# First MLP, parts of five strips, first strip pair: groups behind five plain pieces and two apart, where they stood behind four and three apart

## The chip, the cores and the metric

The kernel runs on one core of a Trainium2 chip (trn2). Five engines work from queues of their own: TensorE (PE) multiplies, VectorE (DVE), ScalarE (ACT) and GpSimd (POOL) work on elements, and SyncE (SP) issues most DMAs. They wait for each other through semaphores. The metric is the device time of one execution in microseconds (us).

## What is computed

The reference chains two blocks over 256 tokens of width 2048, all in fp32. The change lies in the MLP of the first block, in its second matrix:

```python
def sq_relu_mlp(h, w1, w2):
    return jnp.square(jax.nn.relu(h @ w1)) @ w2

# first_block, DEPTH = 1, D_MODEL = 2048, D_FF = 8192:
    h = h + y                                   # y: attention with stick-breaking weights
    h = h + sq_relu_mlp(rms_norm(h, norm_mlp[i]), mlp_w1[i], mlp_w2[i])
return rms_norm(h, final_norm)
# second_block: local attention and pooling, then a gated MLP with a convolution (w_up, w_down)
```

## The kernel before

**Pieces.** Every weight matrix is cut into pieces of 256 rows by 512 columns. A *plain* piece is loaded into one of six `raw` buffers (512 KB). ACT copies it to `Wh`, rounded to the matrix format (the high half, line 1132), and DVE subtracts to get `Wl`, the low half (line 1356). The activations lie there as high and low halves too. PE then issues three products for each of 2 row halves and 2 blocks of 128 rows: 12 matmuls of 128x512 to a plain piece. The products of a strip (512 columns) add up in one PSUM set, `ps0` or `ps1`.

**Groups.** In a *strip pair*, two neighbouring strips of `mlp_w2`, some rows are done for both strips together, as a product of 2x2 blocks with seven multiplications. The function is `seven`. Such a group stands in the list of pieces as four quarters, q0 to q3 (kinds `s0` to `s3`), with 6, 6, 6 and 3 matmuls. q0 and q1 have a raw buffer each, q2 and q3 have no load of their own: DVE makes them from the two raw buffers, by four sums (lines 1362 to 1367, buffer `wsum`). Mixed tokens (`hidMix`) are the other factor, and part of the result goes to a third PSUM set, `ps2`. When the last group is done, `fold` and `fold_rest` add `ps2` into `xN` on DVE, with one copy on ACT.

**The order.** The planner writes a list of pieces (`p.pieces`) and from it one list of steps, which all engines follow, each with its own part. While PE is at piece i, the piece four further on is split (`LEAD` = 4, there are `NW` = 5 buffers for `Wh` and `Wl`). For q0 that split brings the four sums with it (`sums_and_split`). Jobs put off with `later(n, ...)` come n plain pieces further on; a quarter counts as half a piece, the last one as a quarter of it.

**The first MLP.** The hidden width is done in three parts of 6, 5 and 5 strips. Each part first computes its strips of `mlp_w1`, then multiplies them with its rows of `mlp_w2`, in two strip pairs (s4 = 0 and s4 = 2). A part of five strips has ten pieces of rows; three of them are groups (`sevens`) and seven are plain in each of the two strips, a and b: a0 to a6, b0 to b6. In the first pair the last two of each (a5, a6, b5, b6) stand at the end as a tail (`tail` = 2), as their rows are those of the last hidden strip.

A hidden strip takes a way round before it can be multiplied: ACT takes it out of PSUM with ReLU and squares it (`stage_rows`, lines 1192 and 1200, into `T0`), SP writes it to memory and lands it turned (`land_rows`), DVE transposes it from `T0` to `T1` (`turn_strip`, line 1459), ACT writes its high half (`hid_high`, line 1235), DVE its low half (`hid_low`, line 1524). `T0` is one buffer, so ACT can take the next strip out of PSUM only behind the transpose of the one before. In the first pair, a3 and a4 read the fourth hidden strip of the part (tiles 12 to 15), the tail reads the fifth.

**Where the groups stand.** `strip_pair` puts `lead` plain pieces of strip a first, and then groups with `gap` plain pieces between them:

```python
lead, gap = (lead or 4, 3 if lead is None or len(plain) > 7 else 2) if tail else (lead or 2, 3 if len(plain) > 7 else 2)
rest = a[lead:n] + b[:n] if tail else a[lead:n - 1] + b[:lead] + a[n - 1:] + b[lead:]
```

For the first pair of a part of five strips (no `lead` given, seven plain pieces, n = 5) this gives a0 a1 a2 a3, group, a4 b0 b1, group, b2 b3 b4, group, a5 a6 b5 b6.

Of the kernel before, what the change touches and what calls it, by code (L numbers as in the profile page):

```python
# [26 lines left out]
class Plan:  # L27
# [7 lines left out]
    def done(self, name, by=1):  # L35

        if name not in self.sems:
            self.sems[name], self.count[name] = self.sem(f"s_{name}"), 0
        self.count[name] += by
        return self.sems[name], self.count[name]  # L40

    def step(self, kind, **kw):
        self.steps.append(dict(kind=kind, **kw))
        return self.steps[-1]

    def after(self, i, job, ahead=False):
        jobs = self.later_steps.setdefault(i, [])
        jobs.insert(0 if ahead else len(jobs), job)

    def later(self, n, job):  # L50

        i, left = self.at, 4 * n
        while left > 0:
            i += 1
            left -= QUARTERS.get(self.pieces[i]["kind"], 4) if i < len(self.pieces) else 4
        self.after(i, job)


def plan_program(sem):
# [34 lines left out]
    def strip(w, col, ks, mov, tiles, evac, koff=0):  # L94
        first = len(p.pieces)
        strips[0] += 1
        for n, kp in enumerate(ks):
            src = (w, "rows", kp * 256, col)
            p.pieces.append(dict(src=src, shape=2, mov=mov, kt=2 * (kp - koff), tiles=tiles, kind="N", first=n == 0,
                                 start=(n == 0, n == 0), last=n == len(ks) - 1, evac=evac, early=None, strip=strips[0]))  # L100
        return first

    def strip_pair(w, s4, ks, tail, mov, tiles, evacs, koff=0, sevens=(), fold=None, lead=None):

        plain = [kp for kp in ks if kp not in sevens]
        first, n = len(p.pieces), len(plain) - tail
        for i in range(2):
            strip(w, (s4 + i) * STRIP, plain, mov, tiles, evacs[i], koff)
        a, b = p.pieces[first:first + len(plain)], p.pieces[first + len(plain):]
        if not sevens:  # L110
            p.pieces[first:] = a[:n] + b[:n] + a[n:] + b[n:]
            return first
        b[0]["first"], b[0]["start"] = False, (False, True)
        lead, gap = (lead or 4, 3 if lead is None or len(plain) > 7 else 2) if tail else (lead or 2, 3 if len(plain) > 7 else 2)
        rest = a[lead:n] + b[:n] if tail else a[lead:n - 1] + b[:lead] + a[n - 1:] + b[lead:]
        p.pieces[first:] = a[:lead]
        for m, kp in enumerate(sevens):
            seven(w, s4, kp, mov, tiles, (a[0]["strip"], b[0]["strip"]), koff, m, m == 0, fold if m == len(sevens) - 1 else None)
            p.pieces += rest[gap * m:gap * m + gap] if m < len(sevens) - 1 else rest[gap * m:]
        p.pieces += a[n:] + b[n:] if tail else []  # L120
        order = [q["strip"] if q["kind"] == "N" else 0 for q in p.pieces[first:]]
        assert max(j for j, k in enumerate(order) if k == 0) < max(j for j, k in enumerate(order) if k == a[0]["strip"])
        assert min(j for j, k in enumerate(order) if k == 0) < min(j for j, k in enumerate(order) if k == b[0]["strip"])
        return first
# [43 lines left out]
    def fold_into(to, s4, fresh=False):  # L168

        def f(sets, k):  # L170
            copied = done("fold_copied")
            marks = [done("folded") for i in range(5 if fresh else 8)]
            step("fold", to=to, s4=s4, k=k, sums_free=list(free["sums"]), copied=copied, marks=marks, fresh=fresh)

            def second():
                step("fold_rest", to=to, s4=s4, marks=marks, fresh=fresh)
                free["sums"], free["set2"] = [marks[-1]], [marks[-1]]
                st["fold", s4], st["fold", s4 + 1] = marks[-1], marks[-1]
                taken.clear()
            later(1, second)  # L180
        return f
# [8 lines left out]
    def row_norm(into):  # L190

        total, mean, root = done("row_total"), done("rms_mean"), done("rms_root")
        rec, sq, prod, r = done("rms_rec"), done("rms_rec"), done("rms_rec"), done("rms_r")
        step("row_norm", need=st["rows_sq"], total=total, mean=mean, root=root, rec=rec, sq=sq, prod=prod, r=r)
        st[into] = r
# [168 lines left out]
    for g in range(4):  # L364
        at = first["v", g] + (7 if g else 12)
# [4 lines left out]
    def evac_rows(s4, gain_name=None, more=None):  # L370
        def f(s, k):
            added = [done("rows_added") for t in range(2)]
            step("add_products", s4=s4, set=s, mm=k, x_rows=x_rows[-1], folded=st.pop(("fold", s4), None), done=added)
            free[f"set{s}"] = [added[1]]
            if gain_name == "mlp":
                row_squares(s4, added)
                move_rows(s4, "mlp", added)
            if gain_name == "pre2":
                apart = 1 if s4 < 2 else 0

                def squared():
                    sq = row_squares(s4, added)
                    later(1 + apart, lambda: gained(sq))

                def gained(sq):
                    g = [done("rows_gained") for t in range(2)]
                    step("gain_rows_x", n=s4, need=sq, row=st["final_row"], done=g)
                    st["final_used"] = g[1]
                    if s4 < 3:
                        move_rows(s4, "pre2", g, 5 - (s4 == 2))  # L390
                    else:
                        later(2, lambda: turn(s4, "pre2", g))
                    if apart:
                        later(1, lambda: row_squares(s4, g, gained=True))
                    else:
                        row_squares(s4, g, gained=True)
                if apart:
                    later(1, squared)
                else:
                    squared()  # L400
            if more:
                more(s, k[1])
        return f
# [7 lines left out]
    def evac_relu(t0, mixed):  # L411
        n = next_trip()

        def f(s, k):
            def landed(moved):
                turned = done("hid_turned")
                step("turn_strip", to="T1", need=[moved, *free["T1"]], done=turned)
                free["T0"], free["T1"] = [turned], [turned]
                later(1, lambda: high(turned))

            def high(turned):
                hi, lo = done("hid_hi"), done("hid_lo")
                step("hid_high", t0=t0, need=turned, hi=hi)
                free["T1"] = [lo]
                later(1, lambda: low(turned, hi, lo))

            def low(turned, hi, lo):
                step("hid_low", t0=t0, hi=hi, lo=lo)
                if mixed and t0 < 8:
                    free["T1"] = [lo, mix_tokens("hid1", "T1", t0 // 2, 2 if t0 == 0 else 1, [turned])]  # L430
                hid_tiles[t0:t0 + 4] = [lo] * 4
            trip(s, k, n, "relu", "b", [st["r2"]], landed, 5)
        return f
# [14 lines left out]
    at = 0  # L448
    for c, n in enumerate((6, 5, 5)):
        for j in range(n):  # L450
            i = strip("mlp_w1", (at + j) * STRIP, ALL8, "aHL", tile_hl, evac_relu(4 * j, True))
            if at + j == 0:
                after(i + 3, lambda: row_norm(into="r2"))
        for s4 in (0, 2):
            evacs = [evac_rows(s4 + m, "pre2" if c == 2 else None, load_bias if c == 2 and s4 + m == 3 else None)
                     for m in range(2)]
            i = strip_pair("mlp_w2", s4, tuple(range(2 * at, 2 * (at + n))), 0 if s4 else 2, "hid1", hid_tiles, evacs, koff=2 * at,
                           sevens=() if c == 2 and s4 else tuple(range(2 * at, 2 * at + 3)), fold=fold_into("xN", s4))
            if c == 1 and s4 == 0:
                after(i, final_row)  # L460
        at += n
# [278 lines left out]
    at = 0  # L740
    for c, n in enumerate((6, 5)):
# [5 lines left out]
        for s4 in (0, 2):  # L747
            i = strip_pair("w_down_2", s4, tuple(range(2 * at, 2 * (at + n))), 0 if s4 else 2, "hid2", hid_tiles,
                           [evac_y(c, s4), evac_y(c, s4 + 1)], koff=2 * at,
                           sevens=(2 * at, 2 * at + 1, 2 * at + 4) if c == 0 or s4 == 0 else (),  # L750
                           fold=fold_into("xn", s4, fresh=c == 0), lead=4 if s4 else 2 * n - 5)
# [1262 lines left out]
```

## Time and profile before

| | |
|---|---|
| median of three runs | 2083.42 us (2083.16 to 2085.51) |
| profiled execution | 2083.09 us |
| its span, first to last instruction | 2081.4 us |
| PE busy | 2069.7 us, 99% of the span |
| DVE, ACT busy | 1387.0 us (67%), 1126.7 us (54%) |
| DMA | 226 GB/s on the mean |
| chain that ended last | PE 96%, DVE 2%, ACT 1% |

The page gives busy time by engine. In a timeline a row is one instruction, or several like ones merged (x2): start, duration, engine, line of the kernel, operation, output and inputs; in brackets the idle time of the engine before it and what ended that. Matmuls overlap: one is shown with 0.39 us, and the next starts 0.23 us after it.

### The profile page before, as it was taken

The numbers are of one execution on the slowest core, as the hardware profiler recorded it, in microseconds if no ns is written. First come the engines' busy times: TensorE is split into PE (matmuls) and PEld (weight loads), VectorE is DVE, ScalarE is ACT, GpSimd is POOL, SyncE is SP. The second block draws the span as 40 slices with busy tenths as digits, with TensorE's granted clock in tenths as the row PEclk, the third lists the DMA queues.
The fourth block names the chain that finished last, engine by engine and source line by source line (L and its number), as shares of the span: only waits on it lengthen the run. The fifth ranks groups of instructions, "written<-read, shape, count | busy, mean of one in ns | idle before, by whom it ended". The sixth has DMA issues, their size and how long they took to land.

```text
span 2081.4 us, 24042 instructions
## 1 busy us (share of the span) xinstructions
PE 2069.7 (99%) x9232; PEld 1713.9 (82%) x9232; DVE 1387.0 (67%) x1574; ACT 1126.7 (54%) x1369; POOL 59.9 (3%) x55
## 2 busy tenths in 40 slices
PE   9999999999999999999999999999999999999998
PEld 8888888888888888888888888888888888888877
DVE  6546555665884669666876655566766885576795
ACT  7555554555554555455655544455555554555563
POOL 3000000000000000000002000000000000000010
PEclk9999999999999999999999999999999999999999
DMA  8687656787657775777677787667787666777853
GB/s 297 197 255 232 190 187 218 253 235 254 219 188 222 231 245 201 226 222 245 222 254 239 219 249 228 199 207 222 245 249 239 203 213 212 238 226 246 259 192 142
DMA packets 291907, 469.50 MB, mean 226 GB/s; under 512 B 18512, under 2 KB 82128, under 8 KB 291280
## 3 DMA queue, kind: packets, MB, share of 16 engines
q1 hardware_dynamic: 290928, 463.46, 70.8%
q10 hardware_dynamic: 864, 4.49, 0.7%
q8 instruction: 73, 1.20, 0.2%
q14 instruction: 42, 0.34, 0.0%
HBM read 432.75 MB, written 35.13 MB: 225 GB/s over the span
## 4 chain that ended last, share of the span: by engine, by line
PE 96%; DVE 2%; ACT 1%; issue 0%; DMA 0%; ACTq 0%; DVEq 0%
PE ps L1752 96%; DVE Wl L1356 1%; ACT Wh L1132 0%; DVE E L1615 0%; DVE T L1459 0%; PE ps L1755 0%; ACT E L1276 0%; DMA gains<-in_gains_dram 0%; ACT T L1192 0%; DVE hid L1524 0%; ACT hid L1235 0%; DVE wsum L1367 0%; DVE E L1621 0%; DVE wsum L1362 0%; ACT L1110 0%
## 5 line engine op out<-in xcount | busy, mean ns | idle before, releaser
L1356 DVE TENSOR_TENSOR Wl<-raw,Wh 128x1024 fp32r<-128x1024 f32 x743 | 909.1, 1243 | 568.7 <-ACT Wh L1132 562.0
L1752 PE MATMUL ps<-Wh,aHL 128*128 128x512 f32 x3712 | 1148.7, 390 | 0.7 <-ACT aHL L1160 0.4
L1132 ACT ACTIVATE Wh<-raw 128x1024 fp32r<-128x1024 f32 x743 | 770.5, 1056 | 538.8 <-PE ps L1752 505.3
L1752 PEld LDWEIGHTS ps<-Wh,aHL 128*128 128x128 f32 x3712 | 696.7, 188 | 146.4 <-issue 1.7
L1752 PE MATMUL ps<-Wl,aHL 128*128 128x512 f32 x1856 | 722.1, 389 | 0.0
L1752 PE MATMUL ps<-Wh,hid 128*128 128x512 f32 x1488 | 464.8, 390 | 3.1 <-DVE Wl L1356 2.3
L1752 PEld LDWEIGHTS ps<-Wl,aHL 128*128 128x128 f32 x1856 | 348.4, 188 | 71.6
L1752 PEld LDWEIGHTS ps<-Wh,hid 128*128 128x128 f32 x1488 | 279.3, 188 | 64.4 <-DVE Wl L1356 3.3
L1752 PE MATMUL ps<-Wl,hid 128*128 128x512 f32 x744 | 289.5, 389 | 0.0
L1752 PEld LDWEIGHTS ps<-Wl,hid 128*128 128x128 f32 x744 | 139.7, 188 | 28.9
L1752 PE MATMUL ps<-Wh,oHL 128*128 128x512 f32 x512 | 159.0, 390 | 0.0
L1752 PEld LDWEIGHTS ps<-Wh,oHL 128*128 128x128 f32 x512 | 96.1, 188 | 19.9
L1752 PE MATMUL ps<-Wl,oHL 128*128 128x512 f32 x256 | 99.6, 389 | 0.0
L1195 ACT ACTIVATE T<-ps,rs 128x512 f32<-128x512 f32 x72 | 46.5, 684 | 75.5 <-DVE T L1459 53.3
L1752 PE MATMUL ps<-Wh,hidMix 128*128 128x512 f32 x192 | 63.0, 389 | 0.0
L1132 ACT ACTIVATE Wh<-wsum 128x1024 fp32r<-128x1024 f32 (+1 forms) x48 | 40.1, 841 | 31.2 <-PE ps L1752 30.1
L1752 PEld LDWEIGHTS ps<-Wl,oHL 128*128 128x128 f32 x256 | 48.1, 188 | 9.9
L1356 DVE TENSOR_TENSOR Wl<-wsum,Wh 128x1024 fp32r<-128x1024 f32 (+1 forms) x48 | 44.1, 952 | 4.8 <-ACT Wh L1132 4.8
L1459 DVE STREAM_TRANSPOSE T<-T 128x1024 f32<-128x1024 f32 x38 | 47.1, 1240 | 0.0
L1752 PEld LDWEIGHTS ps<-Wh,hidMix 128*128 128x128 f32 x192 | 36.0, 188 | 7.5
L1192 ACT ACTIVATE T<-ps,rs 128x512 f32<-128x512 f32 x32 | 20.5, 685 | 34.3 <-DVE T L1459 32.5
L1752 PE MATMUL ps<-Wl,hidMix 128*128 128x512 f32 x96 | 37.3, 389 | 0.0
(202 smaller groups left out, 921.3 us busy)
## 6 DMA issues: line engine op xcount, KB each, us to landing
raw<-in_mlp_w_dram SPq DMA_DIRECT2D x256, 512.0 KB, 4.8
raw<-in_w_up_dram SPq DMA_DIRECT2D x176, 512.0 KB, 4.6
raw<-in_sb_w_qkv_dram SPq DMA_DIRECT2D x93, 512.0 KB, 5.4
raw<-in_w_down_dram SPq DMA_DIRECT2D x88, 512.0 KB, 5.0
raw<-in_w_in_dram SPq DMA_DIRECT2D x64, 512.0 KB, 5.3
passed_strip<-T SPq DMA_DIRECT2D x104, 256.0 KB, 3.6
T<-passed_strip SPq DMA_DIRECT2D x208, 128.0 KB, 4.6
raw<-in_sb_w_o_dram SPq DMA_DIRECT2D x32, 512.0 KB, 5.1
```

The lines of the kernel that those rows point to most:

```text
L1132: e.activation(Wh[:, i % NW, c], src, ACT.Copy).then_inc(st["hi"][0], 1)
L1192: e.activation(strip_rows[:, t, :], ps[st["set"]][:, t, :], ACT.Relu, scale=cols[st["col"]][:, t:t + 1]).then_inc(st["staged"][t][0], 1)
L1195: e.activation(strip_rows[:, t, :], ps[st["set"]][:, t, :], ACT.Copy, scale=cols[st["col"]][:, t:t + 1]).then_inc(st["staged"][t][0], 1)
L1356: e.tensor_tensor(Wl[:, i % NW, c], src, Wh[:, i % NW, c].bitcast(F32), ALU.subtract).then_inc(st["lo"][0], 1)
L1459: e.transpose(dst, strip_blocks).then_inc(st["done"][0], 1)
L1752: return e.matmul(o, l, r, start=start, stop=stop, skip_group_check=True)
```

## The change

For the second and third part (c = 1 and 2, five strips each), the first strip pair is given `lead` = n = 5. By the line above, `gap` then is 2, not 3, as `lead` is no longer None and the plain pieces are seven:

```diff
             i = strip_pair("mlp_w2", s4, tuple(range(2 * at, 2 * (at + n))), 0 if s4 else 2, "hid1", hid_tiles, evacs, koff=2 * at,
-                           sevens=() if c == 2 and s4 else tuple(range(2 * at, 2 * at + 3)), fold=fold_into("xN", s4))
+                           sevens=() if c == 2 and s4 else tuple(range(2 * at, 2 * at + 3)), fold=fold_into("xN", s4),
+                           lead=n if c and not s4 else None)
```

The list of pieces becomes a0 a1 a2 a3 a4, group, b0 b1, group, b2 b3, group, b4, a5 a6 b5 b6. The part of six strips, the second strip pairs and the second block keep their order. In the changed file every line below the call is numbered one higher.

DVE at the beginning of the first pair, second part; before. The first row turns the fourth hidden strip, the sums are those of the first group, `hid1` is the low half of the fourth strip:

```order
L1459 STREAM_TRANSPOSE T1<-T0 128x1024
L1362 TENSOR_TENSOR wsum<-raw 128x512
L1363 TENSOR_TENSOR raw<-raw 128x512
L1365 TENSOR_TENSOR wsum<-wsum,raw 128x512
L1367 TENSOR_TENSOR wsum<-wsum,raw 128x512
L1356 TENSOR_TENSOR Wl<-raw,Wh 128x1024 x2
L1524 TENSOR_TENSOR hid1<-T1,hid1 128x4x256
L1356 TENSOR_TENSOR Wl<-wsum,Wh 128x1024
L1356 TENSOR_TENSOR Wl<-wsum,Wh 128x512
```

The same place after the change:

```order
L1460 STREAM_TRANSPOSE T1<-T0 128x1024
L1357 TENSOR_TENSOR Wl<-raw,Wh 128x1024
L1363 TENSOR_TENSOR wsum<-raw 128x512
L1364 TENSOR_TENSOR raw<-raw 128x512
L1366 TENSOR_TENSOR wsum<-wsum,raw 128x512
L1368 TENSOR_TENSOR wsum<-wsum,raw 128x512
L1357 TENSOR_TENSOR Wl<-raw,Wh 128x1024
L1525 TENSOR_TENSOR hid1<-T1,hid1 128x4x256
L1357 TENSOR_TENSOR Wl<-raw,Wh 128x1024
L1357 TENSOR_TENSOR Wl<-wsum,Wh 128x1024
L1357 TENSOR_TENSOR Wl<-wsum,Wh 128x512
```

The split of a4 now stands ahead of the four sums, and ahead of `hid1` there are one split, the sums and one split, where there were the sums and two splits.

ACT at the same place, before. The first rows take the fifth hidden strip out of PSUM:

```order
L1192 ACTIVATE T<-ps,rs 128x512 x2
L1200 ACTIVATE T<-T 128x512 x2
L1132 ACTIVATE Wh<-raw 128x1024
L1168 DMA QK<-in_final_norm_dram 128x2048
L1235 ACTIVATE hid<-T 128x4x256
L1132 ACTIVATE Wh<-raw 128x1024
L1132 ACTIVATE Wh<-wsum 128x1024
L1132 ACTIVATE Wh<-wsum 128x512
```

And after:

```order
L1193 ACTIVATE T<-ps,rs 128x512 x2
L1201 ACTIVATE T<-T 128x512 x2
L1133 ACTIVATE Wh<-raw 128x1024
L1169 DMA QK<-in_final_norm_dram 128x2048
L1236 ACTIVATE hid<-T 128x4x256
L1133 ACTIVATE Wh<-raw 128x1024 x2
L1133 ACTIVATE Wh<-wsum 128x1024
L1133 ACTIVATE Wh<-wsum 128x512
```

The rows up to `hid` are the same; the one split between the squares and `hid` was q0's and is now a4's, and behind `hid` stand two splits of raw buffers, q0's and q1's.

DVE at the third group of the same pair, before; its first row turns the fifth hidden strip:

```order
L1459 STREAM_TRANSPOSE T1<-T0 128x1024
L1356 TENSOR_TENSOR Wl<-raw,Wh 128x1024 x3
L1362 TENSOR_TENSOR wsum<-raw 128x512
L1363 TENSOR_TENSOR raw<-raw 128x512
L1365 TENSOR_TENSOR wsum<-wsum,raw 128x512
L1367 TENSOR_TENSOR wsum<-wsum,raw 128x512
L1356 TENSOR_TENSOR Wl<-raw,Wh 128x1024 x2
L1524 TENSOR_TENSOR hid1<-T1,hid1 128x4x256
L1356 TENSOR_TENSOR Wl<-wsum,Wh 128x1024
L1356 TENSOR_TENSOR Wl<-wsum,Wh 128x512
L1356 TENSOR_TENSOR Wl<-raw,Wh 128x1024 x4
```

And after:

```order
L1460 STREAM_TRANSPOSE T1<-T0 128x1024
L1357 TENSOR_TENSOR Wl<-raw,Wh 128x1024 x2
L1363 TENSOR_TENSOR wsum<-raw 128x512
L1364 TENSOR_TENSOR raw<-raw 128x512
L1366 TENSOR_TENSOR wsum<-wsum,raw 128x512
L1368 TENSOR_TENSOR wsum<-wsum,raw 128x512
L1357 TENSOR_TENSOR Wl<-raw,Wh 128x1024 x2
L1357 TENSOR_TENSOR Wl<-wsum,Wh 128x1024
L1525 TENSOR_TENSOR hid1<-T1,hid1 128x4x256
L1357 TENSOR_TENSOR Wl<-wsum,Wh 128x512
L1357 TENSOR_TENSOR Wl<-raw,Wh 128x1024 x4
```

Between the transpose and the sums there are two splits, not three, and the low half of the fifth strip stands behind q2, not ahead of it. In the third part the same rows move in the same way.

## Rows read from the trace of the kernel before

**Rows 1.** The page, busy time by engine (share of the span, instructions).

```profile
PE 2069.7 (99%) x9232; PEld 1713.9 (82%) x9232; DVE 1387.0 (67%) x1574; ACT 1126.7 (54%) x1369; POOL 59.9 (3%) x55
```

**Rows 2.** Waits of PE, whole span: us in total, times, longest.

```profile
PE ps L1752 <- DVE hid L1524: 0.7, 2, 0.4
```

**Rows 3.** Timeline (start, us, engine, line, operation) of PE; last row: third part.

```profile
749.61 0.39 PE L1752 MATMUL ps<-Wh,hid 128*128 128x512 f32 x1
...
757.54 0.39 PE L1752 MATMUL ps<-Wh,hid 128*128 128x512 f32 x1
758.30 0.50 PE L1752 MATMUL ps<-Wh,hid 128*128 128x512 f32 x1 [0.37 <-DVE hid L1524]
758.64 0.40 PE L1752 MATMUL ps<-Wl,hid 128*128 128x512 f32 x1
...
972.53 0.50 PE L1752 MATMUL ps<-Wh,hid 128*128 128x512 f32 x1 [0.37 <-DVE hid L1524]
```

**Rows 4.** Timeline of DVE, beginning of the second part's first pair.

```profile
749.38 1.24 DVE L1459 STREAM_TRANSPOSE T<-T 128x1024 f32<-128x1024 f32 x1
750.54 0.65 DVE L1362 TENSOR_TENSOR wsum<-raw 128x512 f32<-128x512 f32 x1
...
752.43 0.69 DVE L1367 TENSOR_TENSOR wsum<-wsum,raw 128x512 f32<-128x512 f32 x1
753.99 1.23 DVE L1356 TENSOR_TENSOR Wl<-raw,Wh 128x1024 fp32r<-128x1024 f32 x1 [0.87 <-ACT Wh L1132]
755.88 1.23 DVE L1356 TENSOR_TENSOR Wl<-raw,Wh 128x1024 fp32r<-128x1024 f32 x1 [0.67 <-ACT Wh L1132]
757.03 1.22 DVE L1524 TENSOR_TENSOR hid<-T,hid 128x1024 fp32r<-128x1024 f32 x1
```

**Rows 5.** Timeline of ACT, the same stretch.

```profile
750.71 1.27 ACT L1192 ACTIVATE T<-ps,rs 128x512 f32<-128x512 f32 x2 [2.50 <-DVE T L1459]
...
752.90 1.05 ACT L1132 ACTIVATE Wh<-raw 128x1024 fp32r<-128x1024 f32 x1
753.85 1.06 ACT L1235 ACTIVATE hid<-T 128x1024 fp32r<-128x1024 f32 x1
754.80 1.05 ACT L1132 ACTIVATE Wh<-raw 128x1024 fp32r<-128x1024 f32 x1
```

**Rows 6.** Timeline of DVE, third group of the same pair.

```profile
778.71 1.23 DVE L1356 TENSOR_TENSOR Wl<-raw,Wh 128x1024 fp32r<-128x1024 f32 x1 [0.67 <-ACT Wh L1132]
779.85 0.69 DVE L1362 TENSOR_TENSOR wsum<-raw 128x512 f32<-128x512 f32 x1
...
782.38 2.36 DVE L1356 TENSOR_TENSOR Wl<-raw,Wh 128x1024 fp32r<-128x1024 f32 x2
784.65 1.22 DVE L1524 TENSOR_TENSOR hid<-T,hid 128x1024 fp32r<-128x1024 f32 x1
...
785.79 1.82 DVE L1356 TENSOR_TENSOR Wl<-wsum,Wh 128x1024 fp32r<-128x1024 f32 x2
```

**Rows 7.** Timeline of DVE, beginning of the third part's first pair.

```profile
968.22 1.23 DVE L1356 TENSOR_TENSOR Wl<-raw,Wh 128x1024 fp32r<-128x1024 f32 x1 [0.87 <-ACT Wh L1132]
...
971.26 1.22 DVE L1524 TENSOR_TENSOR hid<-T,hid 128x1024 fp32r<-128x1024 f32 x1
```

**Rows 8.** Timeline of SP, fifth hidden strip landing, second part.

```profile
761.98 1.81 SPq L1057 DMA_DIRECT2D T<-passed_strip  x4
```

**Rows 9.** Timelines of DVE and PE, second MLP's part of five strips.

```profile
1998.11 3.23 DVE L1615 SCALAR_TENSOR_TENSOR E<-T,conv,E 128x255 f32<-128x255 f32 x8
...
2003.25 0.50 PE L1752 MATMUL ps<-Wh,hid 128*128 128x512 f32 x1 [1.28 <-DVE Wl L1356]
```

**Rows 10.** Stretches: length, busy time of engines (count), granted clock, DMA share, GB/s.

```profile
2076.00:2077.50 1.50, 1.12 (x2) 0.30 (x2) 1.50 (x3) 0.28 (x2) 0.00 (x0) 0.96 0.13 52
...
2002.00:2003.25 1.25, 0.00 (x0) 0.00 (x0) 1.25 (x3) 0.62 (x1) 0.00 (x0) 1.00 0.01 3
```

## Prediction

> **What bounds the kernel now.** I read the page first: TensorE (PE) is busy for 2069.7 us of a span of 2081.4 us [rows 1]. So only time in which PE stands still can be won, and time in which it is made to stand still is lost in full. The waits of PE over the whole span come next [rows 2]: the sum for products that read `hid` is small, 0.7 us for two waits on the operation that writes its low half (line 1524). The listing of PE's waits by time puts one of them into each of the two places that the change touches: at 758.30 us (first part of five strips) and at 972.53 us (second) [rows 3].
>
> What PE waits for at 758.30: it starts piece a0 at 749.61 and issues 36 matmuls (a0, a1, a2) until 757.54; 35 steps in 7.93 us are 0.2266 us each, so a plain piece of 12 is 2.72 us [rows 3]. a3 is due at 749.61 + 3 x 2.72 = 757.77, and starts at 758.30. It is the first piece that reads hidden tiles 12 to 15 of this part, and their low half, on VectorE (DVE) at 757.03, takes 1.22 us, to 758.25 [rows 4]. The loss is 0.53 us, of which the wait row shows 0.37 (a matmul's modelled end runs past the next start), and some 0.11 us for the first step after the pause, 0.34 instead of 0.23 [rows 3].
>
> What holds DVE before that is the point. Its sequence from 749.38 is: transpose, the four sums for the first group (750.54 to 753.12), low half of q0 (753.99), low half of q1 (755.88), then `hid` (757.03) [rows 4]. Both low halves wait for ScalarE (ACT), 0.87 and 0.67 us. ACT meanwhile is copying and squaring the last strip of the hidden layer out of PSUM; it starts on that at 750.71, when the transpose has freed its buffer, and only then makes the high half of the next piece (752.90), `hid`'s high half (753.85) and the next one (754.80) [rows 5]. So **the four sums lie in the shadow of ACT's copying**, 2.58 us that cost nothing today.
>
> **The change part by part.** No instruction is added or removed on any engine: the same 14 plain pieces and three groups run, in another order, so PE's own work is the same (cost nothing). What moves, twice in the program:
>
> 1. *The first group goes behind a4.* The fifth piece of the pair to be split is now a4, a plain piece, and not q0. On ACT nothing changes up to the high half of the second piece: it is a copy of one raw buffer in either order, 752.90 to 753.95. On DVE, by the order of the changed kernel, the low half of a4 now stands ahead of the four sums, and it cannot start before ACT's copy at 753.95. So the sums leave the shadow. From 753.99 on: low half of a4, 1.14 us to the next instruction (778.71 to 779.85); four sums, 2.53 us (779.85 to 782.38); low half of q0, 1.14 us (half of 784.65 - 782.38) [rows 6]. `hid`'s low half starts at 753.99 + 1.14 + 2.53 + 1.14 = 758.80 and ends 1.22 later, at 760.02; its high half (ended 754.91) and q0's high half (the next on ACT, where today's q1 stands, 754.80 to 755.85) are there long before [rows 5]. PE gets 0.05 us after that, as today: **760.07 instead of 758.30, 1.77 us later**. In short: 4.81 us from the low half to `hid` instead of today's 757.03 - 753.99 = 3.04.
>
> 2. *The same in the second part.* The distance there is the same: the low half to `hid` takes 3.04 us there too (968.22 to 971.26) [rows 7]. Another 1.77 us. **Sum of both: 3.54 us.**
>
> The sum rests on DVE waiting in its order. The trace shows that it does: for 0.67 us up to 755.88 DVE stood idle for the low half of q1, while `hid`, next in its order, had its input since 754.91 [rows 4, 5]. The Trainium skill (TensorE: Matmul & The Clock Gate, "Architectural detail: the array is 16× 32×32, not 1× 128×128") says the same against this change, that ScalarE and VectorE work strictly first in, first out: by the rule the sum is 3.54 us, and for an engine that took ready sums first it would be 0. The trace agrees with the rule, by the 0.67 us just named.
>
> 3. *Groups two plain pieces apart.* DVE's work for a group and two plain pieces is 2.53 (sums) + 2.27 (q0, q1) + 1.82 (q2, q3) + 2 x 1.14 = 8.9 us; PE needs 21 + 24 matmuls of 0.2266, 10.2 us [rows 3, 6]. That fits, with a transpose (1.24) or a `hid` (1.14) in between just about [rows 4, 6]. Carried on from 760.07, PE would be at the first group at 765.7, b0 at 770.4, second group 775.9, third group 786.1, b4 at 790.8. DVE would be busy without a gap from the low half of b0 (about 767.0) on, and have each low half ready 2 to 2.6 us ahead of PE: b0 ready 768.2, q0 of the third group 783.2 (the transpose of the last strip and four splits lie ahead), b4 at 788.4. Bounds of what it costs: below nothing it cannot go, since PE does not wait there today (no row of PE waiting between 758.30 and 972.53); above, 1.28 us a place, from the nearest rows (rival B); I take 0, since the count leaves 2 us.
>
> 4. *The last strip of the hidden layer.* Its `hid` moves behind q2 of the third group, some 0.7 us later (785.87 to about 786.6), and PE wants it at the tail, 791.8 today, 793.5 then [rows 6]. 5.9 us of cover become 6.9: nothing. On the SP queue the four landings of that strip are now behind three loads of weights instead of two; the third waits for q1's low half at about 761.1. Today they start at 761.98 [rows 8], and the transpose that needs them is due on DVE only at about 776: nothing.
>
> 5. *The fold after the groups.* It begins one plain piece earlier, and the sums for the second strip pair's first group get more room. PE does not wait there today, so this gains nothing.
>
> Total: the profiled execution took 2083.09 us (span 2081.4 us, 1.7 us around it), so 2086.63 us. The median of the three runs is 0.33 us higher, 2083.42, so **2086.96 us**, 0.17% more. I call 0.2% (4.2 us) the least that a measurement of this kernel can tell from no change; the forecast lies just under it.
>
> **The rivals.** *A, the forecast*: one longer wait for `hid` at a3 in each of the two places.
>
> *B, new waits between the groups*, on top of A. For: the second MLP's part of five strips has this very layout (five pieces ahead, two apart), and PE waits there 1.28 us for a low half [rows 9]. Against: there DVE does eight convolution steps ahead of it, 3.23 us [rows 9]; here it is one transpose or one `hid`, and I find 2 us of reserve. It decides if DVE comes 2 us later than I count. Price 1.28 a place: 2086.96 + 2.56 = 2089.5 us.
>
> *C, not slower*: ACT makes a4's high half ahead of its copying, not behind. It stands idle for 2.50 us up to 750.71 [rows 5], and a4's buffer is free once PE has left the last piece of the layer before, at 749.6. Then the low half of a4 would follow the transpose at 750.6, the sums end at 754.3, and `hid` could start at about 755.4 and end at 756.7, before a3 is due at 757.77: both waits would be gone, 0.53 + 0.11 us each, 2083.42 - 1.3 = 2082.1 us. Against: ACT's order in the changed kernel has the copying first. It decides by whether that high half starts before 750.71 or at 752.90. That the change does not do what it says is ruled out by the order of the changed kernel, which shows it at both places.
>
> *D, the clock.* PE's pause at a3 grows from 0.37 to 2.1 us. Through the pause of 1.28 us in the second MLP the granted clock stayed at 1.00 (2.4 GHz), and behind the longest, at the very end, it reads 0.96 [rows 10]. If it fell to 1.2 GHz and one piece ran at that, it would take 2.72 us more, twice: 2092.4 us. The Trainium skill (TensorE: Matmul & The Clock Gate, "HAM oscillation — how this bites in real kernels") says that pauses between bursts can send TensorE back to the lower clock; the rows so far show none of that at pauses like this one.
>
> **How the numbers follow.** A 0.78, B 0.10, C 0.08, D 0.02, and 0.02 for a gain that I have not seen. A's own spread is that of the runs, 2083.16 to 2085.51 for the same kernel, and a tenth or two in the hand count: 2085.4 to 2088.5. The range leaves out C and D, takes in A and comes near B: 2085.4 to 2089.2 us. Faster by over 0.2% would need 4.2 us, and all that PE loses to these two waits is 1.3: 0.02. Slower by over 0.2%: B, D, and of A the sixth or so that scatter lifts over 2087.6: 0.25. Within 0.2%: 0.73.
>
> **What would show it.** In the changed kernel's timeline, PE waits for `hid` about 2.1 us at some 760.07 and 974.30 us, and PE's total wait on line 1524 goes from 0.7 to 4.3 us. On DVE the four sums start near 755.1, not 750.5, behind a low half at 753.99. No other wait of PE between there and 860 us. B shows as PE waits for a low half (line 1356 of before) near 770 to 791; C as sums or the low half of a4 right behind the transpose; D as a granted clock below 1.00 around 760. The forecast is wrong if PE's wait at a3 is not near 2.1 us, or if its waits add up to something else than the change in time.

## The result and the profile after

| | before | after |
|---|---|---|
| median of 15 runs | 2083.37 us (2082.83 to 2085.51) | 2088.64 us (2086.73 to 2091.33) |
| profiled execution | 2083.09 us | 2088.79 us |
| its span | 2081.4 us | 2087.0 us |

The ratio is 1.0026, with a 95% interval of 1.0018 to 1.0034: the change makes the kernel slower, by 5.27 us, and the slowest run of the kernel before is under the fastest of the changed one. The prediction was 2086.96 us, 3.54 us more than before. The longer wait that it describes is there, to a few hundredths of a microsecond. The other 1.7 us come from D, the fall of the clock, to which it gave 0.02.

**The waits of PE** over the span of the changed kernel (total us, times, longest), the largest two; they answer to [rows 2]. The wait for `hid` went from 0.7 to 4.3 us, and the wait for low halves stands where it stood, four times and 2.4 us beside 2.3 (the last row is that of the kernel before), so no wait between the groups came with the change:

```profile
PE ps L1753 <- DVE hid L1525: 4.3, 2, 2.1
PE ps L1753 <- DVE Wl L1357: 2.4, 4, 1.3
...
PE ps L1752 <- DVE Wl L1356: 2.3, 4, 1.3
```

**The timeline of PE** of the changed kernel, to be laid beside [rows 3]: a0 of the second part, a3 there, a3 in the third part, and the start of a strip some 383 us further on.

```profile
750.20 0.39 PE L1753 MATMUL ps<-Wh,hid 128*128 128x512 f32 x1
...
760.66 0.50 PE L1753 MATMUL ps<-Wh,hid 128*128 128x512 f32 x1 [2.14 <-DVE hid L1525]
...
976.64 0.50 PE L1753 MATMUL ps<-Wh,hid 128*128 128x512 f32 x1 [2.15 <-DVE hid L1525]
...
1359.83 0.47 PE L1753 MATMUL ps<-Wh,aHL 128*128 128x512 f32 x1 [0.44 <-ACT aHL L1161]
```

The last of these in the kernel before:

```profile
1354.09 0.47 PE L1752 MATMUL ps<-Wh,aHL 128*128 128x512 f32 x1 [0.44 <-ACT aHL L1160]
```

Row by row, the distance to the kernel before: a0 starts 750.20 - 749.61 = 0.59 us later, which has grown up ahead of the place that was changed and is no part of it. From a0 to a3 it is 10.46 us instead of 8.69: **1.77 us**, the term of step 1. From there to a3 of the third part 215.98 instead of 214.23: **1.75 us**, step 2. From there to 1359.83 it is 383.19 instead of 381.56: **1.63 us that no wait of PE accounts for**.

**DVE** at the beginning of the pair, beside [rows 4]. The sums have left the shadow of ACT's copying: DVE stands idle for 3.37 us, then does a low half, the sums, another low half, and only then `hid`.

```profile
749.97 1.24 DVE L1460 STREAM_TRANSPOSE T<-T 128x1024 f32<-128x1024 f32 x1
754.58 1.23 DVE L1357 TENSOR_TENSOR Wl<-raw,Wh 128x1024 fp32r<-128x1024 f32 x1 [3.37 <-ACT Wh L1133]
755.72 0.69 DVE L1363 TENSOR_TENSOR wsum<-raw 128x512 f32<-128x512 f32 x1
...
757.65 0.69 DVE L1368 TENSOR_TENSOR wsum<-wsum,raw 128x512 f32<-128x512 f32 x1
758.25 1.22 DVE L1357 TENSOR_TENSOR Wl<-raw,Wh 128x1024 fp32r<-128x1024 f32 x1
759.39 1.22 DVE L1525 TENSOR_TENSOR hid<-T,hid 128x1024 fp32r<-128x1024 f32 x1
```

From the first low half to `hid` it is 759.39 - 754.58 = 4.81 us, where [rows 4] have 3.04.

**DVE at the third group**, beside [rows 6]: from the low half of b0 on (the first row) it is busy but for two gaps of some 0.2 us, which the merged rows of 2.59 and 2.58 us hold. `hid` of the last strip stands behind q2, and PE has no wait here.

```profile
767.61 2.59 DVE L1357 TENSOR_TENSOR Wl<-raw,Wh 128x1024 fp32r<-128x1024 f32 x2 [2.46 <-ACT Wh L1133]
...
777.82 2.58 DVE L1357 TENSOR_TENSOR Wl<-raw,Wh 128x1024 fp32r<-128x1024 f32 x2
...
782.84 2.35 DVE L1357 TENSOR_TENSOR Wl<-raw,Wh 128x1024 fp32r<-128x1024 f32 x2
785.12 1.22 DVE L1357 TENSOR_TENSOR Wl<-wsum,Wh 128x1024 fp32r<-128x1024 f32 x1
786.25 1.22 DVE L1525 TENSOR_TENSOR hid<-T,hid 128x1024 fp32r<-128x1024 f32 x1
```

**The clock.** Stretches of the changed kernel (length, busy time of PE, its weight loads, DVE, ACT and POOL with counts, granted clock, DMA share, GB/s). The first two are the pause at a3 of the second part and what comes behind it, the others the same in the third part:

```profile
758.40:760.60 2.20, 0.12 (x1) 0.00 (x0) 2.20 (x3) 1.06 (x1) 0.00 (x0) 1.00 1.01 385
760.60:764.20 3.60, 3.54 (x15) 2.92 (x16) 2.28 (x3) 0.40 (x1) 0.00 (x0) 1.00 0.69 216
974.40:976.60 2.20, 0.10 (x1) 0.00 (x0) 2.20 (x3) 1.06 (x1) 0.00 (x0) 1.00 0.20 60
976.60:977.90 1.30, 1.25 (x5) 1.05 (x6) 1.30 (x2) 0.00 (x0) 0.00 (x0) 1.00 0.79 249
977.90:981.50 3.60, 3.60 (x10) 2.79 (x9) 0.96 (x1) 0.53 (x1) 0.00 (x0) 0.54 0.75 228
981.50:984.00 2.50, 2.50 (x12) 2.07 (x11) 0.69 (x1) 0.10 (x1) 0.00 (x0) 0.99 0.80 162
```

Behind the pause in the third part the granted clock is 1.00 for 1.3 us, then 0.54 for 3.6 us (the level of 1.2 GHz), then 0.99. Behind the pause of the same length in the second part it stays at 1.00. The matmuls of that stretch show what it costs:

```profile
977.67 0.40 PE L1753 MATMUL ps<-Wl,hid 128*128 128x512 f32 x1
977.91 0.83 PE L1753 MATMUL ps<-Wh,hid 128*128 128x512 f32 x2
978.53 0.63 PE L1753 MATMUL ps<-Wl,hid 128*128 128x512 f32 x1
978.96 1.05 PE L1753 MATMUL ps<-Wh,hid 128*128 128x512 f32 x2
...
981.52 0.65 PE L1753 MATMUL ps<-Wh,hid 128*128 128x512 f32 x2
```

A row with a single matmul is followed by the next start after 0.24 us at 977.67 and after 0.43 us at 978.53. From 977.91 on, up to the one at 981.52, nine matmuls start (the rows hold two and one in turn, three times over); at 0.2266 us [rows 3] they would take 2.04 us, and they take 3.61. That is 1.57 of the 1.63 us.

The 15 runs lie in three heaps: 2086.73 and 2086.91; eight from 2088.16 to 2088.79; five from 2089.90 to 2091.33. From heap to heap the medians are 1.6 and 2.0 us apart, near the price of one such fall, so the heaps read as runs with a fall behind none, one or both of the two pauses. The profile shows that for one execution of the middle heap. The granted clock on the mean of the span, on record for every run, bears out a part of it for the others: it is 0.999 in the two runs of the lowest heap, as in the 58 runs of the kernel before that lie beside the experiments, and 0.998 in the other 13. With three decimals it does not tell one fall from two; that rests on the times. The forecast, 2086.96, is the heap without a fall.

### The profile page after: what moved, and what is told of

Read it like the earlier page. It is cut to its first block, busy times and chain, and to the rows that moved or that the text cites. A ratio compares the mean times of both kernels' runs of the same rounds, so it can differ in the third digit from the quotient of the medians.

```text
span 2087.0 us, 24042 instructions
## 1 busy us (share of the span) xinstructions
PE 2071.6 (99%) x9232; PEld 1715.3 (82%) x9232; DVE 1385.9 (66%) x1574; ACT 1127.5 (54%) x1369; POOL 60.2 (3%) x55
## 4 chain that ended last, share of the span: by engine, by line
PE 96%; DVE 2%; ACT 1%; issue 1%; DMA 0%; ACTq 0%; DVEq 0%
PE ps L1753 96%; DVE Wl L1357 1%; ACT Wh L1133 0%; DVE E L1616 0%; DVE T L1460 0%; PE ps L1756 0%; ACT E L1277 0%; DMA gains<-in_gains_dram 0%; DVE wsum L1368 0%; DVE wsum L1363 0%; ACT T L1193 0%; DVE wsum L1366 0%; DVE raw L1364 0%; DVE hid L1525 0%; DVE E L1622 0%
```

## The experiments

Two questions were put. First, what makes the wait: S, the sums that left the shadow of ACT's copying, ahead of `hid` on DVE, or the groups that stand closer together. Second, what takes the remaining 1.7 us: the clock (D), or something in the order of the pieces that no wait shows. The first four kernels ran beside a median of 2083.48 us of the kernel before (31 runs), the last four beside 2083.37 us (27 runs). In the diffs "..." stands for code that is left out.

### The two halves of the change apart

The first kernel keeps the groups behind five pieces, but three apart:

```diff
-lead, gap = (lead or 4, 3 if lead is None or len(plain) > 7 else 2) if tail else ...
+lead, gap = (lead or 4, 3 if lead is None or len(plain) > 7 or w == "mlp_w2" else 2) if tail else ...
```

> Half of the change alone: the groups begin behind five plain pieces, but stay three apart. Theory S (the four sums of the first group have left the shadow of ScalarE's copying): the whole loss is here, PE waits 2.1 us for hid at a3 in both places, 2086.9 us without a fall of the clock and some 1.6 us more for each pause behind which the clock falls, so 2086.8, 2088.4 or 2090.1 us by run. Rival G (the groups two apart crowd VectorE, and the loss comes from there): as before, 2083.4 us, waits of 0.37 us.

Measured: 2088.86 us (2086.62 to 2090.91, nine runs), ratio 1.0024 (1.0014 to 1.0033). Its waits of PE, and a stretch of its third part:

```profile
PE ps L1753 <- DVE hid L1525: 4.3, 2, 2.1
...
PE ps L1753 <- DVE aHL L1500: 0.8, 1, 0.8
```

```profile
978.00:982.00 4.00, 4.00 (x13) 3.15 (x12) 1.73 (x2) 0.00 (x0) 0.00 (x0) 0.60 0.80 239
```

The whole loss comes with the five pieces ahead, waits and fall of the clock alike. The heaps that were expected are less clear here: one run at 2086.62 us (mean clock 0.999), seven from 2088.31 to 2089.61 and one at 2090.91 (0.998 in all eight). The wait of 0.8 us for `aHL` is somewhere else, and in none of the other profiles; it stays unexplained, and the profiled execution, with 2089.61 us, is the slowest of the seven.

The second kernel is the kernel before with the groups two apart, behind four pieces:

```diff
-lead, gap = (lead or 4, 3 if lead is None or len(plain) > 7 else 2) if tail else ...
+lead, gap = (lead or 4, 2 if w == "mlp_w2" and len(plain) == 7 else 3 if lead is None or len(plain) > 7 else 2) if tail else ...
```

> The other half alone: behind four plain pieces as before, but two apart. Theory S: as before, 2083.4 us, PE waits 0.37 us for hid at a3 in each place and nowhere else in the pair, the clock does not fall. Rival G: 2086 to 2089 us, with new waits of PE between the groups.

Measured: 2083.38 us (2082.99 to 2083.72, 11 runs), ratio 0.9999 (0.9990 to 1.0008), and the wait for `hid` is that of [rows 2]:

```profile
PE ps L1752 <- DVE hid L1524: 0.7, 2, 0.4
```

Two apart costs nothing that can be measured, and PE has no other wait from 740 to 1100 us. Step 3 stands, and rival B falls.

### The sums put back into the shadow

The changed kernel, with the four sums issued ahead of a4's split instead of behind it. Piece i + n is q0 of the first group, and `sums` holds the four sums, which `sums_and_split` then leaves out:

```diff
@@ strip pairs of the first MLP
+            if c and s4 == 0:
+                p.pieces[i + n]["ahead"] = True
...
@@ split of a plain piece
         elif i < N:
+            if i + 1 < N and p.pieces[i + 1].get("ahead"):
+                sums(i + 1)
             step("split", i=i, part="N", ...)
```

> The changed kernel with one thing put back: VectorE makes the four sums of the first group ahead of a4's low half, right behind the transpose, where ScalarE's copying covers them. Pieces in the changed order. Theory S: hid ends 1.77 us earlier again, waits of PE 0.4 us instead of 2.1, no fall of the clock, 2083.4 us. Rival L (it is the late first group or the order of pieces itself, whatever VectorE does ahead of hid): stays at 2086.8 to 2090 us.

Measured: 2083.45 us (2082.91 to 2084.21, 11 runs), ratio 1.0000 (0.9991 to 1.0008). DVE at the place, with the same 0.87 and 0.67 us of idling as in [rows 4]:

```profile
751.06 0.65 DVE L1373 TENSOR_TENSOR wsum<-raw 128x512 f32<-128x512 f32 x1
...
754.51 1.23 DVE L1367 TENSOR_TENSOR Wl<-raw,Wh 128x1024 fp32r<-128x1024 f32 x1 [0.87 <-ACT Wh L1143]
756.40 1.23 DVE L1367 TENSOR_TENSOR Wl<-raw,Wh 128x1024 fp32r<-128x1024 f32 x1 [0.67 <-ACT Wh L1143]
757.55 1.22 DVE L1535 TENSOR_TENSOR hid<-T,hid 128x1024 fp32r<-128x1024 f32 x1
```

The pieces stand in the order of the changed kernel, and all of the loss is gone, the 1.7 us that no wait shows included. The mean clock is 0.999 in all 11 runs. So S holds, and those 1.7 us hang on the pause, not on the order of the pieces.

### The low half of `hid` ahead of the sums

In the changed kernel the low half of the fourth hidden strip is called right behind its high half, not put off by one piece (`fourth` is set for j = 3 in the parts c = 1 and 2):

```diff
@@ evac_relu
-                later(1, lambda: low(turned, hi, lo))
+                if fourth:
+                    low(turned, hi, lo)
+                else:
+                    later(1, lambda: low(turned, hi, lo))
```

> The changed kernel with the low half of the fourth hidden strip moved ahead on VectorE: right behind a4's low half, in front of the four sums. Theory S: hid starts at about 755.1 and ends at 756.4 in the times of the kernel before, 1.4 us ahead of a3, so both waits are gone: the 0.53 us a place lost before are won as well, 2083.4 - 1.3 = 2082.1 us, and the clock stays at 1.00. Rival P (the pause only moves on, to q0 of the first group, whose low half then comes later): some 1 us of wait there in each place, 2084 us.

Measured: 2081.88 us (2081.51 to 2082.05, 11 runs), ratio 0.9991 (0.9982 to 1.0000). PE has no wait for `hid` left. DVE:

```profile
753.98 1.23 DVE L1360 TENSOR_TENSOR Wl<-raw,Wh 128x1024 fp32r<-128x1024 f32 x1 [3.37 <-ACT Wh L1136]
755.12 1.22 DVE L1528 TENSOR_TENSOR hid<-T,hid 128x1024 fp32r<-128x1024 f32 x1
756.26 0.69 DVE L1366 TENSOR_TENSOR wsum<-raw 128x512 f32<-128x512 f32 x1
```

This is the fastest kernel of the study, 1.60 us under the kernel before, and its slowest run (2082.05) is under the fastest of the 31 runs beside it (2082.95). DVE's sums no longer lie ahead of what PE needs first. The same edit in the kernel before, where the groups begin behind four pieces:

> The kernel before with the same move of the low half of the fourth hidden strip alone: right behind q0's low half, ahead of q1's. If the gain of the run with that move in the changed kernel is the two waits and nothing of the order of pieces, this gives the same 2081.9 us, PE without any wait for hid. If the order of pieces has a part in it, they differ: by up to 1 us.

Measured: 2082.17 us (2081.84 to 2082.68, 11 runs), ratio 0.9994 (0.9985 to 1.0003), no wait for `hid` either; 1.20 us under the kernel before. The interval takes in no change, but the slowest run (2082.68) is under the fastest of the 27 beside it (2082.86). With the wait gone, the order of the groups makes 0.3 us of difference or none: the two kernels ran beside different medians, and their gains lie within each other's intervals.

### Other lengths of the pause

If the clock takes the rest, a shorter pause should cost its length and no more, and a longer one more than its length. In the next kernel (the changed one) the low half stands behind the sums, ahead of q0's low half:

```diff
@@ evac_relu
-                later(1, lambda: low(turned, hi, lo))
+                if fourth:
+                    p.behind_sums = lambda: low(turned, hi, lo)
+                else:
+                    later(1, lambda: low(turned, hi, lo))
...
@@ sums_and_split, behind the four sums
+            if p.behind_sums:
+                p.behind_sums()
+                p.behind_sums = None
```

> The changed kernel with the low half of the fourth hidden strip between the four sums and q0's low half: one low half (1.14 us) earlier than in the changed kernel. PE waits 1.0 us instead of 2.14 at a3, in both places: 2083.45 + 2 x 0.63 = 2084.7 us. Theory K (the clock falls the more often the longer the pause): no fall here, as behind the pauses of 1.28 us, all runs within 2084.3 to 2085.3. Rival (any pause for hid at these places can bring the fall): some runs 1.6 or 3.3 us above.

Measured: 2084.69 us (2084.11 to 2085.29, 11 runs), ratio 1.0007 (0.9998 to 1.0015). The wait, and the stretches of both pauses with what follows each:

```profile
PE ps L1759 <- DVE hid L1531: 2.0, 2, 1.0
```

```profile
758.00:759.10 1.10, 0.09 (x2) 0.04 (x1) 1.10 (x2) 0.95 (x1) 0.00 (x0) 1.00 1.01 391
759.10:762.50 3.40, 3.40 (x15) 2.83 (x16) 3.31 (x3) 0.44 (x2) 0.00 (x0) 1.00 0.65 234
972.90:973.90 1.00, 0.02 (x1) 0.02 (x1) 1.00 (x2) 0.93 (x1) 0.00 (x0) 1.00 0.28 107
973.90:977.50 3.60, 3.60 (x16) 2.98 (x17) 3.33 (x3) 0.63 (x2) 0.00 (x0) 1.00 0.31 98
```

The two pauses are 1.01 us each, 2 x (1.01 - 0.37) = 1.28 us more than before, and the time is 1.32 us more: the pause costs itself, and the clock stays at 1.00. All 11 runs lie within 1.2 us, in one heap, each with a mean clock of 0.999.

In the next one the low half is put off by two pieces instead of one, behind q1's low half:

```diff
-                later(1, lambda: low(turned, hi, lo))
+                later(2 if fourth else 1, lambda: low(turned, hi, lo))
```

> The changed kernel with the low half of the fourth hidden strip one low half later, behind q1's: PE waits 3.28 us at a3 in both places, 2083.45 + 2 x 2.91 = 2089.3 us with the clock at 1.00. Theory K: the clock falls behind both pauses in nearly every run, at 1.6 us each, so 2092.5 us and runs closer together than those of the changed kernel. Rival (the fall does not go by the length): the same mix of none, one and two falls as in the changed kernel, 2089.3, 2090.9 and 2092.5.

Measured: 2092.19 us (2091.78 to 2093.51, five runs), ratio 1.0045 (1.0032 to 1.0057). The wait, and the stretches from the pause on, of the second part and then of the third; the profiled execution took 2093.28 us:

```profile
PE ps L1753 <- DVE hid L1525: 6.6, 2, 3.3
```

```profile
757.90:761.20 3.30, 0.06 (x1) 0.00 (x0) 3.30 (x4) 1.06 (x1) 0.00 (x0) 0.86 0.95 346
761.20:767.00 5.80, 5.76 (x14) 4.56 (x15) 1.12 (x1) 0.17 (x1) 0.00 (x0) 0.50 0.94 226
977.70:981.00 3.30, 0.11 (x1) 0.00 (x0) 3.30 (x4) 1.06 (x1) 0.00 (x0) 1.00 0.37 123
981.00:982.20 1.20, 1.11 (x5) 0.92 (x6) 1.17 (x2) 0.00 (x0) 0.00 (x0) 0.98 0.85 239
982.20:985.50 3.30, 3.30 (x9) 2.58 (x8) 0.00 (x0) 0.00 (x0) 0.00 (x0) 0.50 1.02 235
```

In this execution both pauses bring the fall to 1.2 GHz, the one still within the pause (0.86), the other 1.1 us behind it. The starts of PE, laid beside those of the kernel before as above, put the price of the first fall at 2.7 us and of the second at 1.6:

```profile
761.24 0.80 PE L1753 MATMUL ps<-Wh,hid 128*128 128x512 f32 x1 [3.28 <-DVE hid L1525]
...
981.09 0.50 PE L1753 MATMUL ps<-Wh,hid 128*128 128x512 f32 x1 [3.28 <-DVE hid L1525]
...
1364.26 0.47 PE L1753 MATMUL ps<-Wh,aHL 128*128 128x512 f32 x1 [0.44 <-ACT aHL L1161]
```

From 761.24 to 981.09 it is 219.85 us, 5.62 more than 214.23; 2.91 of that is the longer wait of the third part, 2.71 are left. From there to 1364.26 it is 383.17, 1.61 more than 381.56. The waits alone are 2 x (3.28 - 0.37) = 5.82 us, so 2089.2 us; all five runs are 2.6 to 4.3 us above that, with a mean clock of 0.997. That is one long fall or two in each; only the profiled execution shows which. A pause of 3.28 us in place of one of 0.37 costs 4.2 to 5.1 us on the mean of the two places, falls included.

The last kernel makes the change in the second part alone:

```diff
-                           lead=n if c and not s4 else None)
+                           lead=n if c == 1 and not s4 else None)
```

> The change in the second part alone, the third as before. One pause of 2.14 and one of 0.37 us: 2083.45 + 1.77 = 2085.2 us where the clock stays, 2086.8 where it falls, two clusters of runs 1.6 us apart, and none near 2088.5. Rival (falls come in the third part alone): one cluster at 2085.2.

Measured: 2086.59 us (2084.57 to 2089.66, 11 runs), ratio 1.0015 (1.0006 to 1.0024). The waits at a3, one long and one as before:

```profile
760.32 0.50 PE L1753 MATMUL ps<-Wh,hid 128*128 128x512 f32 x1 [2.14 <-DVE hid L1525]
...
974.50 0.50 PE L1753 MATMUL ps<-Wh,hid 128*128 128x512 f32 x1 [0.37 <-DVE hid L1525]
```

One longer wait is 2083.37 + 1.77 = 2085.14 us, one fall more 2086.77. Four runs lie from 2084.57 to 2085.41, six from 2086.57 to 2087.58. The mean clock is 0.999 in the four, 0.998 in five of the six. So the times and clocks say that the second part's pause brings the fall too, in about half of the executions, though neither this kernel's profile (2085.15 us, the lower heap) nor that of the changed kernel happened to catch it there. Two runs are left open: 2089.66 us (0.998) fits neither heap, and 2087.58 us has 0.999.

## Why the prediction was right, and where it fell short

**Steps 1 and 2 are right**, term by term: 4.81 us from the low half to `hid` were predicted and measured, 1.77 us a place were predicted and 1.77 and 1.75 measured. The kernel with the sums put back shows that this is the cause, and not only the place. The step rested on DVE waiting in its order, and it does. Of the 2.5 us of sums only 1.77 show up, as some 0.7 us of them now fill the time in which DVE stood idle for q1's high half before.

**Steps 3, 4 and 5 are right.** The groups two apart cost nothing by themselves (2083.38 beside 2083.48 us), no wait came up between them, DVE is busy nearly all the time from the low half of b0 on, and `hid` of the last strip behind q2 makes nobody wait. One slip in step 3 changes nothing: its own figures put the low halves 2.2 to 2.9 us ahead of PE, not 2 to 2.6. B is out by the waits, and C by the DVE rows: a4's low half waits 3.37 us for ACT instead of following the transpose.

**The step that failed is the weighing of D.** The mechanism was named, with its sign, and then given 0.02, because through the 1.28 us pause of [rows 10] the clock stayed at 1.00. But that pause is shorter than the 2.1 us which step 1 had just worked out. The runs agree with the row and not with what was drawn from it: at 1.01 us there is no fall, at 2.14 us there is one in many executions, at 1.6 us a fall. The other row there, 0.96, stands behind the one pause of such a length in the trace of the kernel before:

```profile
2076.13 1.12 PE L1752 MATMUL ps<-QK,zs 128*128 128x512 f32 x2 [2.25 <-ACT zs L1300]
```

It could not decide either way, as only these two matmuls follow: they end at 2077.25, and in finer stretches the clock is 1.00 up to 2077.2 and 0.50 from 2077.4 on. Whether the pause or the end of the work brought that fall can't be told. So the rows left D open at 2.1 us, and 0.02 was not worked out from them.

The Trainium skill (TensorE: Matmul & The Clock Gate, "HAM oscillation — how this bites in real kernels") says that pauses between bursts can send TensorE to the lower clock; the trace of the changed kernel agrees in this, with 0.54 behind a pause of 2.15 us, shorter than the waits in that section's example.

**D's price was off too, the other way.** One piece at half speed, 2.72 us in each place, was the guess. The fall in the profile of the changed kernel lasts 3.6 us and costs 1.63. That, once or twice in most runs, lifts the median from A's 2086.96 to 2088.64 us. It is why "within 0.2%" looked likelier than "slower", while the measured 0.26% is past that line.

**That the time lies in the range is luck.** The range ended at 2089.2 us, while A's own spread, by the prediction, ended at 2088.5. The room above that was left for B, which did not come; D took it, at less than the price that was set on it. And by one of the prediction's own signs the forecast is wrong: PE's waits for `hid` add up to 3.6 us more, and the time is 5.27 us more.

**Open:** why the same pause of 2.14 us brings the fall in one execution and not in the next, and in one execution at one of the two places and not at the other; and the runs at 2087.58 and 2089.66 us.

## What to carry to other kernels

An edit that moves a group of steps moves what they bring along: four sums of 2.5 us were free while their engine waited for another one, and cost 1.8 us a place as soon as an instruction that waits for that other engine stood ahead of them. Look for the instruction that the bound engine needs first and ask what stands ahead of it in its queue; calling `hid`'s low half one step earlier is worth 1.2 to 1.6 us against the kernel before, in either order of the groups. And where TensorE is made to stand still, look for a pause of the same length in the trace, and not a shorter one, with as much work behind it, before its clock is left out of the sum; where there is none, the clock stays an open term.

## What the runs showed of the hardware that was not expected

- A pause of about 2.1 us in a TensorE that is otherwise busy all along can bring its clock from 2.4 to 1.2 GHz, and the fall comes late: in the profile of the changed kernel 1.3 us after the matmuls have begun again. By the times and clocks of the runs, most executions with two such pauses have a fall (13 of 15). At 1.01 us it was not seen in 11 runs; at 3.28 us it stands behind both pauses of the profiled execution, and the times of all five runs call for at least one fall in each.
- A fall costs 1.6 us behind the 2.15 us pause, nearly as much as the longer wait itself adds (1.75 us). Behind the 3.28 us pause in the second part it lasts for more than 5.8 us and costs 2.7.
